# VectorE takes over the four weight sums of FFN 2's second seven-product unit, and GpSimd holds its sums of the third

## The reference, cut to what matters

```python
h = modulate(rms_norm(x, norm_ffn2[l]), mod[:, 2, 0], mod[:, 2, 1])
x = x + 0.5 * mod[:, 2, 2][:, None, :] * swiglu(h, w_ffn2_in[l], w_ffn2_out[l])
# swiglu: g, u = split(h @ w_in, 2);  (silu(g) * u) @ w_out     with D_FF = 2816
```

## Time and profile before

| | |
|---|---|
| median of 3 runs | 1037.24 us (1036.77 to 1037.76) |
| the profiled execution's own time | 1036.71 us |
| its span | 1034.9 us |
| PE busy | 1008.1 us (97%) |
| DVE busy | 773.0 us (75%) |
| ACT busy | 459.5 us (44%) |
| POOL busy | 284.7 us (28%) |
| POOL's L2384, first of the four sums | x30, mean 1739 ns |

### The profile page before, as it was taken

One profiled execution on the slowest core, in us unless ns is written; L12 is line 12 of the kernel. 1 busy time (PEld: TensorE's weight loads), 2 busy tenths in 40 slices (PEclk: granted clock), 3 DMA queues, 4 the chain that ended last, 5 costly groups with the idle time before them and its releaser, 6 DMA issues.

```text
span 1034.9 us, 15026 instructions
## 1 busy us (share of the span) xinstructions
PE 1008.1 (97%) x6078; PEld 907.3 (88%) x6078; DVE 773.0 (75%) x1055; ACT 459.5 (44%) x711; POOL 284.7 (28%) x167
## 2 busy tenths in 40 slices
PE   3999999999999999999999999999999999999998
PEld 2888888899998899898888888899999889999987
DVE  5887876789997975777766677589999438999722
ACT  6632323345453234577655553465554214455311
POOL 0000000557851200640000001305683025778000
PEclk9999999999999999999999999999999999999999
DMA  9778865332227722132212214111322232323231
GB/s 360 298 281 318 280 233 179 129 122 97 109 83 261 286 95 103 56 122 82 82 41 81 81 51 165 71 42 46 119 104 104 91 128 86 114 90 108 90 117 73
DMA packets 28914, 139.14 MB, mean 134 GB/s; under 512 B 3248, under 2 KB 3504, under 8 KB 21168
## 3 DMA queue, kind: packets, MB, share of 16 engines
q1 hardware_dynamic: 28848, 138.23, 37.7%
HBM read 136.12 MB, written 2.10 MB: 134 GB/s over the span
## 4 chain that ended last, share of the span: by engine, by line
PE 94%; DVE 2%; DMA 1%; ACT 1%; SPq 1%; issue 1%; DVEq 0%; ACTq 0%
PE bank L533 31%; PE bank L534 30%; PE bank L535 30%; DMA ada_first<-w_ada 1%; PE bank L975 1%; PE bank L956 1%; PE bank L906 0%; DVE k_lo L2028 0%; DVE sx_lo L1753 0%; PE bank L640 0%; DVE w_lo L1753 0%; PE bank L553 0%; DVE h_lo L1641 0%; SPq L477 0%; SPq L482 0%
## 5 line engine op out<-in xcount | busy, mean ns | idle before, releaser
L533 PE MATMUL bank<-h_hi,w_hi 128*128 128x256 f32 (+1 forms) x836 | 278.8, 333 | 3.1 <-DVE h_lo L1788 2.9
L534 PE MATMUL bank<-h_hi,w_lo 128*128 128x256 f32 (+1 forms) x836 | 276.5, 331 | 0.0
L535 PE MATMUL bank<-h_lo,w_hi 128*128 128x256 f32 (+1 forms) x836 | 276.4, 331 | 0.0
L533 PEld LDWEIGHTS bank<-h_hi,w_hi 128*128 128x128 f32 x836 | 159.3, 191 | 18.6 <-DVE h_lo L1788 3.3
L535 PEld LDWEIGHTS bank<-h_lo,w_hi 128*128 128x128 f32 x836 | 159.3, 191 | 14.8
L534 PEld LDWEIGHTS bank<-h_hi,w_lo 128*128 128x128 f32 x836 | 159.4, 191 | 14.1
L2384 POOL TENSOR_TENSOR sx_sum<-w_raw 128x512 f32<-128x512 f32 x30 | 52.2, 1739 | 351.7 <-DMA w_raw<-w_ffn_in 251.2
L533 PE MATMUL bank<-f_hi,w_hi 128*128 128x512 f32 (+1 forms) x374 | 141.1, 377 | 0.0
L534 PE MATMUL bank<-f_hi,w_lo 128*128 128x512 f32 (+1 forms) x374 | 140.8, 377 | 0.0
L535 PE MATMUL bank<-f_lo,w_hi 128*128 128x512 f32 (+1 forms) x374 | 140.8, 376 | 0.0
L1753 DVE TENSOR_TENSOR w_lo<-w_raw,w_hi 128x1024 fp32r<-128x1024 f32 x60 | 96.0, 1606 | 12.7 <-ACT w_hi L1160 12.7
(11 more groups left out here) (274 smaller groups left out, 2136.7 us busy)
## 6 DMA issues: line engine op xcount, KB each, us to landing
w_raw<-w_ffn_in SPq DMA_DIRECT2D x40, 1024.0 KB, 4.8
ada_raw<-w_ada SPq DMA_DIRECT2D x56, 512.0 KB, 5.8
w_raw<-w_ffn_out SPq DMA_DIRECT2D x32, 704.0 KB, 4.1
w_raw<-w_mix SPq DMA_DIRECT2D x19, 1024.0 KB, 4.8
ada_first<-w_ada SPq DMA_DIRECT2D x16, 512.0 KB, 12.8
w_raw<-w_ffn_in SPq DMA_DIRECT2D x6, 512.0 KB, 12.7
x_tok<-x_rows SPq DMA_DIRECT2D x4, 512.0 KB, 6.2
x<-x_t SPq DMA_DIRECT2D x4, 512.0 KB, 5.3
```

The costliest lines, as they stand in the source:

```text
L533: nc.tensor.matmul(dst, a_hi, b_hi, start=start, stop=False)
L534: nc.tensor.matmul(dst, a_lo, b_hi, start=False, stop=False)
L535: return nc.tensor.matmul(dst, a_hi, b_lo, start=False, stop=stop)
```

## The change: what it does

VectorE gets a new function, `second_sums`, called once behind `token_low_last(1)` and ahead of the first unit: it makes the four sums of the second unit (e = 1), with the same operands in the same order and the same counts in `sum_made`. GpSimd's loop over FFN 2's further units starts at e = 2. Ahead of the loop GpSimd now also waits until the second unit's sums are made and until the last `lo` of the second unit's item is made (`item_lo` at `pieces(1, 2)`).

```diff
+            def second_sums():
+
+                n = UNIT_FROM[1] + 1
+                s, count = item_landed(1, 1)
+                dve.wait_ge(landed[s], count)
+                dve.wait_ge(sum_made, 4 * n)
+                raw, sx = ([tile[s][:, at * QUART:at * QUART + QUART] for at in range(size)]
+                           for tile, size in ((w_raw, 4), (sx_sum, 3)))
+                nc.vector.tensor_tensor(sx[2], raw[0], raw[2], ALU.subtract).then_inc(sum_made, 1)
+                dve.wait_ge(sum_made, 4 * n + 1)
+                nc.vector.tensor_tensor(raw[2], raw[2], raw[3], ALU.add).then_inc(sum_made, 1)
+                dve.wait_ge(sum_made, 4 * n + 2)
+                nc.vector.tensor_tensor(sx[0], raw[2], raw[0], ALU.subtract).then_inc(sum_made, 1)
+                dve.wait_ge(sum_made, 4 * n + 3)
+                nc.vector.tensor_tensor(sx[1], raw[1], sx[0], ALU.subtract).then_inc(sum_made, 1)
...
                 act_low(1, 1, 1)
                 token_low_last(1)
+                second_sums()
                 for i in range(ITEMS[1]):
...
             squares_up(2)
             pool.wait_ge(t_done, 15)
-            for e in range(1, UNITS[1]):
+            pool.wait_ge(sum_made, 4 * (UNIT_FROM[1] + 2))
+            pool.wait_ge(item_lo, pieces(1, 2))
+            for e in range(2, UNITS[1]):
                 sums(1, e)
```

## The result

The changed kernel takes 1039.15 us in the median of 20 runs (1038.62 to 1039.96), the kernel before 1037.24 us (20 runs, 1036.14 to 1038.26). The ratio is 1.0020, 95% interval 1.0014 to 1.0026: slower by 1.9 us, where 1037.3 and "no change" were forecast. The profiled execution has a span of 1037.5 us.

A forecast was written before the change was run, and what follows sets the result against it. TensorE was taken to be busy but for 2.42 us in nine units, waiting on VectorE's late queue. Terms -1.55 + 1.7 - 0.1 = about +0.1 gave 1036.8 profiled, 0.53 more for the median: 1037.3 us, range 1035.9 to 1038.6.

The forecast's parts named there:

- Bounds, and who is late: First nine units: TensorE idles 2.42 us in all; VectorE's queue is late, its instructions lengthened by turns with GpSimd.
- Four sums on VectorE, queue up to the pair: Second unit: sums cost 2.84 us, the pair is made at 721.2, TensorE's third part starts 1.55 us sooner.
- GpSimd's wait and the third item's pair: Third unit: held GpSimd's later sums meet the one and the pair, made at 733.0 to 733.1; +1.7 us.
- TensorE stands 1.7 us and restarts at 733.1 + 0.1.: Third unit: TensorE's wait for the pair costs its length plus 0.1 us restart, against 732.98 before; +1.7 us.
- the 73 that I had set as a sign of being wrong: Units three to nine: a stage over 73 us would show the forecast wrong; 72.4 expected, 70.8 before.
- From the fourth unit on: Later units: the old rhythm returns and small idle times, 0.24 us in all, are already paid; 0.1 taken back.
- GpSimd too late: Rival, third unit: GpSimd starts or finishes later, the pair comes 0.5 to 1.6 us later; +0.6 to +1.7; chance 0.16.
- The turns stay: Rival: two more collisions in every unit, VectorE's cycle becomes 10.5 us; +2.7 us, 1039.9; chance 0.04.
- The gain lives: Rival: item 3's sums come behind the pair, the third unit doesn't wait; -1.3 us, 1036.0 (1037.2 if taken back); chance 0.12.

The follow-up runs named there:

- experiment 6: The kernel before, GpSimd still making item 1's sums but then waiting for item 1's last low ahead of item 2's; no sums on VectorE: 1038.20 us, ratio 1.0006.
- experiment 1: The changed kernel with 12 more matmuls into an unread PSUM bank ahead of the third unit's wait for its pair: 1037.85 us, ratio to before 1.0006.
- 3: The changed kernel with only 3 added matmuls (0.36 us) ahead of the third unit's wait: 1037.23 us.
- experiments 5: The changed kernel without GpSimd's wait on `item_lo`; VectorE's four sums stay: 1036.54 us, ratio to before 0.9995.
- 12: The changed kernel without the `item_lo` wait, and with each token low ahead of its activation low in VectorE's queue: 1035.59 us, ratio to before 0.9985.
- experiment 11: The changed kernel with each token low ahead of the activation low beside it in VectorE's queue: 1036.40 us, ratio to before 0.9995.
- experiment 4: The changed kernel with 4 more matmuls ahead of the second unit's wait and none in the third's: 1038.86 us, ratio to before 1.0012.

## Why the prediction was wrong

*Bounds, and who is late.* Right. VectorE's queue was the late one, and taking the turns away from token_low_last and two lows moved the pair.

*Four sums on VectorE, queue up to the pair.* Right to a tenth. Less 0.77, the sums start at 713.17 (said 713.2), the pair is made at 721.24 (721.2), and the second unit ends at 728.59 (728.55).

*GpSimd's wait and the third item's pair.* Right in kind. Less 0.77, item 3's sums begin at 728.90 (said 728.9), the one takes 1.79 and the pair 1.69 us. The pair is made at 733.41, where I said 733.0 to 733.1: GpSimd's fourth sum of item 2 ended at 728.94, not at 728.7, VectorE's `unit_low` beside it took 1.18 for 0.68 us, and so the one began at 729.40, not at 729.0.

In the trace as it stands the one and the pair end 0.55 and 1.09 us behind the end of the GpSimd sum that was running (731.41 and 733.09), and GpSimd's next sum ends 1.13 us behind the one (731.96): turns again. The Trainium skill's rule of the exclusive lock ("SBUF — State Buffer", its section on ports) is again what the trace shows: 1.79 and 1.69 us for 0.68 and 1.21 beside GpSimd (experiment 6 has the same without VectorE's sums).

*"TensorE stands 1.7 us and restarts at 733.1 + 0.1."* **This step failed.** I priced a wait at its length and 0.1 us, by the row at 722.80, behind which the clock had stayed at 1.00. With that I took the clock to be safe behind another wait about as long, without a word on it: it is in none of the terms, bounds and rivals, though the trace of the kernel before has a fall of its own at 382.6, behind 1.11 us of idle time. Behind the 2.11 us the granted clock fell for 3.4 us. From the third unit's third part to the fourth's it is 745.89 - 734.23 = 11.66 us, and 744.10 - 733.91 = 10.19 in experiment 1: the fall costs 1.47 us. TensorE restarted at 733.46 (734.23 less 0.77), where I said 733.2, and 0.1 + 1.47 + 0.26 = 1.83, for the +1.82 of the nine units. 1.47 is the missing term, 0.3 the mis-sized one. The stage of units three to nine is 74.13 us (13.65 + 60.48), over the 73 that I had set as a sign of being wrong.

The Trainium skill ("TensorE: Matmul & The Clock Gate", its part on the clock gate) says that the throttled clock is the default and that activity releases it. Experiments 1 and 3, in which matmuls in the wait keep the higher clock (PEclk 1.00 for 0.87 in the third unit), agree with that; that the fall came 1.3 us into full work, this sentence doesn't tell.

*From the fourth unit on.* Right in kind: TensorE takes 60.48 us over six units, without any idle, where it took 60.72. I had taken back 0.1 of these 0.24.

*Rivals.* "GpSimd too late" named the right place, but with +0.6 to +1.7 us it stays under the measured +1.9, and its mechanism gives 0.3 of that. "The turns stay" did not come. "The gain lives" is what experiments 5 and 12 make true.

*Open.* Why steps of 2.11 and 2.12 us bring the fall, and 1.90, 1.97 and 1.98, or 2.13 with some work in it, do not, isn't settled by these runs. The length of the wait alone doesn't decide: the fall at 382.6 stands behind a step of 1.43 us and 12 matmuls of one column, and the profiled run of experiment 11 has this same step and no fall. Nor is it settled why 2 of 11 runs of experiment 4 went without, and 13 of 99 of the kernel before.

## What to carry to other kernels

Before you hold an engine back, find what it will run beside when it is let go: here a wait of 3 us for GpSimd moved its next batch onto the two instructions that TensorE needed, and held once more it met them a unit later. Price an idle time of TensorE with the clock behind it, not by its length alone, and don't take its safety from one wait of nearly that length: look through the whole trace for stretches at the lower clock, and at what stands ahead of them. Where work runs at an engine's own pace (10.22 us a unit against 10.08), a gain ahead of it lasts only until that pace has used it up, so place the sums where the other engine is idle and fill that engine's own gaps first.

## What the hardware showed that I had not expected

The clock fell 1.3 us after TensorE was back at work, not in the idle time, and stayed low for 3.4 us of full work. Some 0.36 us of matmuls in a wait of 2.13 us were worth 1.36 us in the nine units of the profiled runs (94.96 to 93.60), 1.9 in the medians of two sessions. And VectorE's lows and GpSimd's sums take turns on SBUF: the one, 0.68 us alone, took 1.76 to 1.80 us beside them in eight kernels.
